# One expert's first matrix loaded by two transfers of 4 MB instead of four of 2 MB

## The reference

```python
u = hf[toks] @ w1[e] + b1[e]            # w1[e]: 1024 x 2048 f32, 8 MB
g_, lin = u[:, :D_FF], u[:, D_FF:]
y = ((lin + 1.0) * g_ * jax.nn.sigmoid(SWIGLU_ALPHA * g_)) @ w2[e] + b2[e]   # w2[e]: 1024 x 1024 f32, 4 MB
```

## Time and profile before

| | |
|---|---|
| median of 3 runs | 1930.34 us (1930.14 to 1932.53) |
| the profiled execution's own time | 1930.87 us |
| its span | 1929.1 us |
| mean granted TensorE clock | 0.992 of full |
| PE busy | 1802.8 us, 93% of the span |
| DVE, ACT, POOL busy | 510.2, 252.6, 111.0 us |
| products with `w1` (L1071) | 2112, which is 33 passes of 64 |
| experts (from the first product with `w1` to the last with `w2`) | 243.97 to 1183.09 us |

### The profile page before, as it was taken

One profiled execution on the slowest core, in us unless ns is written; L12 is line 12 of the kernel. 1 busy time (PEld: TensorE's weight loads), 2 busy tenths in 40 slices (PEclk: granted clock), 3 DMA queues, 4 the chain that ended last, 5 costly groups with the idle time before them and its releaser, 6 DMA issues.

```text
span 1929.1 us, 21701 instructions
## 1 busy us (share of the span) xinstructions
PE 1802.8 (93%) x8583; PEld 1033.3 (54%) x8584; DVE 510.2 (26%) x1032; ACT 252.6 (13%) x519; POOL 111.0 (6%) x148
## 2 busy tenths in 40 slices
PE   6997899999999899899898898989999999899998
PEld 3445733333333233233233234867888888788887
DVE  1237432323222222222132123133110005611000
ACT  1125300110001000000010012013110003211000
POOL 4003600000000000000000001000000000200000
PEclk9998999999999999999999999999999999999999
DMA  9683399979999999999999998430333433444430
GB/s 374 259 264 115 128 405 428 429 305 428 427 429 428 428 429 427 428 429 428 428 428 428 429 428 338 149 113 34 141 131 136 166 135 110 152 153 146 160 131 22
DMA packets 93090, 547.36 MB, mean 284 GB/s; under 512 B 5906, under 2 KB 9186, under 8 KB 65298
## 3 DMA queue, kind: packets, MB, share of 16 engines
q1 hardware_dynamic: 92850, 545.75, 70.2%
q10 hardware_dynamic: 192, 0.92, 0.2%
HBM read 545.60 MB, written 1.05 MB: 283 GB/s over the span
## 4 chain that ended last, share of the span: by engine, by line
PE 62%; DMA 31%; DVE 4%; SPq 1%; issue 1%; ACT 1%; POOL 1%; DVEq 0%; POOLq 0%; ACTq 0%
DMA ring<-in_exp_w 30%; PE ps L1131 20%; PE ps L1230 12%; PE ps L1071 12%; PE ps L753 4%; PE ps L1102 4%; PE ps L943 1%; PE ps L1025 1%; PE ps L1043 1%; PE ps L1265 1%; PE ps L1182 1%; DMA ring<-in_w_in 1%; PE ps L711 1%; DVE arena L2000 1%; SPq L475 0%
## 5 line engine op out<-in xcount | busy, mean ns | idle before, releaser
L1071 PE MATMUL ps<-ring,arena 128*64 128x512 f32 x2112 | 473.9, 595 | 56.5 <-DMA ring<-in_exp_w 56.4
L1131 PE MATMUL ps<-hn,ring 128*128 128x272 f32 (+1 forms) x1536 | 346.5, 388 | 0.0
L1071 PEld LDWEIGHTS ps<-ring,arena 128*64 128x64 f32 x2112 | 148.1, 137 | 362.6 <-issue 240.5
L1131 PEld LDWEIGHTS ps<-hn,ring 128*128 128x128 f32 x1536 | 291.8, 190 | 53.3
L1102 PE MATMUL ps<-arena 128*64 128x512 f32 x1056 | 233.9, 595 | 3.5
L1230 PE MATMUL ps<-arena,ring 128*128 128x272 f32 (+1 forms) x1024 | 228.5, 386 | 1.1 <-DVE arena L1950 1.1
L1230 PEld LDWEIGHTS ps<-arena,ring 128*128 128x128 f32 x1024 | 194.3, 190 | 35.0 <-DVE arena L1950 1.9
L1102 PEld LDWEIGHTS ps<-arena 128*64 128x64 f32 x1056 | 75.2, 137 | 140.9 <-issue 140.6
L1311 ACT ACTIVATE arena<-ps 128x512 f32<-128x512 f32 (+2 forms) x135 | 71.1, 535 | 402.9 <-PE ps L1102 212.2
L1851 DVE TENSOR_SCALAR arena<-ps 128x512 f32<-128x512 f32 x33 | 22.8, 691 | 364.9 <-PE ps L1071 364.9
L1763 DVE TENSOR_SCALAR arena<-arena,rstd 128x64 f32<-128x64 f32 x68 | 18.3, 311 | 304.2 <-PE ps L1071 303.5
(11 more groups left out here) (365 smaller groups left out, 1196.6 us busy)
## 6 DMA issues: line engine op xcount, KB each, us to landing
ring<-in_exp_w SPq DMA_DIRECT2D x128, 2048.0 KB, 24.8
arena<-in_exp_w SPq DMA_DIRECT2D x64, 2048.0 KB, 21.8
ring<-in_mlp_w_up SPq DMA_DIRECT2D x16, 2048.0 KB, 7.5
ring<-in_mlp_w_down SPq DMA_DIRECT2D x16, 2048.0 KB, 7.7
ring<-in_ada_w SPq DMA_DIRECT2D x12, 2048.0 KB, 12.6
ring<-in_sb_w_qkv SPq DMA_DIRECT2D x6, 2048.0 KB, 14.0
ring<-in_w_in SPq DMA_DIRECT2D x5, 2048.0 KB, 9.6
ring<-in_lru_w_in SPq DMA_DIRECT2D x4, 2048.0 KB, 7.9
```

The lines of the kernel that those rows point to most:

```text
L1071: last = mm(bank(2 + part)[64 * h:64 * h + 64, :], lhs, w[:, k % 2, at:at + 512], start=False, stop=(k == C - 1))
L1131: last = mm(bank((n0 + q) % 8)[:, lo:TT], w[:, k, P * q:P * q + P], act[:, k, lo:TT], start=(k == 0), stop=(k == C - 1))
```

## The change

The first matrix of an expert comes in two parts of 512 rows (4 MB). Partition p gets four neighbouring rows in one run of 32 KB, across two neighbouring slots of the ring. So that the two slots of a part stand side by side, the attention block's loads begin at slot 3 (`A_FIRST`), and the `w1` parts begin at slot 0. A part is issued when both quarters of it have been read, PE waits once for each part, and the gathered tokens are ordered in fours instead of twos. `w2` is as it was; its loads are now parts 2 and 3, and both wait for `wout_done` 8 in the case of expert 0, as before.

```diff
-PASS_LOADS = 6
+A_FIRST = 3
+PASS_LOADS = 4
...
-A_AT, A_AMOUNT = slot_amounts(A_LOADS, 0, [0] * RING)
-B_AT, _ = slot_amounts(B_LOADS, A_N, [n + 16 * EXPERTS for n in A_AMOUNT])
+A_AT, A_AMOUNT = slot_amounts(A_LOADS, A_FIRST, [0] * RING)
+assert (A_FIRST + A_N) % RING == 0
+B_AT, _ = slot_amounts(B_LOADS, 0, [n + 16 * EXPERTS * (r % 2 == 0) for r, n in enumerate(A_AMOUNT)])
...
-    return ("w1_parts", p * 4 + (part + 1)) if part < 4 else ("w2_parts", p * 2 + (part - 3))
+    return ("w1_parts", p * 4 + 2 * (part + 1)) if part < 2 else ("w2_parts", p * 2 + (part - 1))
...
-        if part < 4:
-            r = (A_N + part) % RING
-            src = a["exp_w1"][0, ds(expert, 1), 2 * P * part:2 * P * (part + 1), :]
-            sp.dma_start(m.ring[:, r, :], src.rearrange("e (p k) n -> p (e k n)", p=P)).then_inc(s.loaded[r], 16)
+        if part < 2:
+            src = a["exp_w1"][0, ds(expert, 1), 4 * P * part:4 * P * (part + 1), :]
+            dst = m.ring[:, 2 * part:2 * part + 2, :].rearrange("p r n -> p (r n)")
+            sp.dma_start(dst, src.rearrange("e (p k) n -> p (e k n)", p=P)).then_inc(s.loaded[2 * part], 16)
...
-        if part < 4:
-            wait_for(a_freed(A_N + part - RING))
-        elif part == 4:
+        if part < 2:
+            wait_for(a_freed(A_N + 2 * part - RING))
+            wait_for(a_freed(A_N + 2 * part + 1 - RING))
+        elif part == 2:
             sp.wait_ge(s["wout_done"], C)
...
-            r = (A_N + kk) % RING
-            pe.wait_ge(s.loaded[r], expert * 16 + (A_AMOUNT[r] + 16))
-            w = m.ring[:, r, :].rearrange("p (k n) -> p k n", n=2 * FF)
+            if kk % 2 == 0:
+                pe.wait_ge(s.loaded[kk], expert * 16 + (A_AMOUNT[kk] + 16))
+            w = m.ring[:, kk, :].rearrange("p (k n) -> p k n", n=2 * FF)
...
-            copy(h2.rearrange("p (a k d) -> p a d k", a=2, k=2),
-                 bank(4 + 2 * t + half).rearrange("p (a d k) -> p a d k", a=2, k=2), "h2_placed")
+            copy(h2.rearrange("p (k d) -> p d k", k=4),
+                 bank(4 + 2 * t + half).rearrange("p (d k) -> p d k", k=4), "h2_placed")
...
-    v.tensor_copy(m.sh_row.rearrange("p (a k d) -> p a d k", a=2, k=2),
-                  bank(3).rearrange("p (a d k) -> p a d k", a=2, k=2)).then_inc(s["sh_read"], 1)
+    v.tensor_copy(m.sh_row.rearrange("p (k d) -> p d k", k=4),
+                  bank(3).rearrange("p (d k) -> p d k", k=4)).then_inc(s["sh_read"], 1)
```

More of the change, by code:

```diff
@@ L478, in load_part @@
     def load_part(part, expert):
-        if part < 4:
-            r = (A_N + part) % RING
-            src = a["exp_w1"][0, ds(expert, 1), 2 * P * part:2 * P * (part + 1), :]
-            sp.dma_start(m.ring[:, r, :], src.rearrange("e (p k) n -> p (e k n)", p=P)).then_inc(s.loaded[r], 16)
-        else:
-            src = a["exp_w2"][0, ds(expert, 1), 512 * (part - 4):512 * (part - 3), :]
-            sp.dma_start(m.w2[:, part - 4, :],
-                         src.rearrange("e (p k) n -> p (e k n)", p=P)).then_inc(s.w2_loaded[part - 4], 16)
+        if part < 2:
+            src = a["exp_w1"][0, ds(expert, 1), 4 * P * part:4 * P * (part + 1), :]
+            dst = m.ring[:, 2 * part:2 * part + 2, :].rearrange("p r n -> p (r n)")
+            sp.dma_start(dst, src.rearrange("e (p k) n -> p (e k n)", p=P)).then_inc(s.loaded[2 * part], 16)
+        else:
+            src = a["exp_w2"][0, ds(expert, 1), 512 * (part - 2):512 * (part - 1), :]
+            sp.dma_start(m.w2[:, part - 2, :],
+                         src.rearrange("e (p k) n -> p (e k n)", p=P)).then_inc(s.w2_loaded[part - 2], 16)
     for part in range(PASS_LOADS):
-        if part < 4:
-            wait_for(a_freed(A_N + part - RING))
-        elif part == 4:
+        if part < 2:
+            wait_for(a_freed(A_N + 2 * part - RING))
+            wait_for(a_freed(A_N + 2 * part + 1 - RING))
+        elif part == 2:
             sp.wait_ge(s["wout_done"], C)
```

## The result

The changed kernel takes 1942.57 us (median of 7 runs, 1940.01 to 1949.04), the kernel before 1932.53 us (7 runs, 1930.14 to 1938.5). The ratio is 1.0055, with an interval of 1.0036 to 1.0074: slower by 10 us, where 10.6 were forecast. (The forecast counted from 1930.34 us, the median of three executions, and so gave 1940.9.)

The account below looks back on a forecast made before the run. The experts' stage was taken as bound by the DMA transfers, delays at restart and end counting one for one. 1.4 + 3.43 + 3.43 + 3.43 - 2.1 + 1.0 = +10.6 us gave 1940.9 us, range 1935 to 1944.5.

Parts of the forecast that it names:

- experts' start: First experts' loads: third quarter issued later with the fourth, delaying loads behind it to expert 1's end; +1.4 us.
- half behind expert 5's landing: First pass of expert 5: 32 products instead of 16 stand behind its last landing; +3.43 us.
- restart after the double pass: Expert 5's second pass: first ring place comes free after 32 products, not 16, so the load queue restarts later; +3.43 us.
- half behind the last landing: Experts' end: 7.08 us of products instead of 3.65 behind the last landing of `w1`; +3.43 us.
- speed of the stream: Expert loads: fewer packets at 4.3 ns each save 0.07 us an expert, over 31 first matrices; -2.1 us.
- longer last packet: Landings of experts 5 and 31: 16 KB more in the last packet costs 0.5 us each; +1.0 us.
- Rival 3: After expert 5: late restart hidden by PE's waitless stretch from 406 to 545; 1932.2 us; chance 0.04.
- a sign of being wrong: Forecast is wrong if restart doesn't move, queue runs dry in steady state, or cadence moves over 0.1 us.
- rival 2: Expert stream and kernel get faster; tie at 0.41 us saved a matrix, 1913.6 us at 450 GB/s; chance 0.05.
- rivals 1 and 4: Expert loads: 1, runs cut into 16 KB packets, 1942.0 us, chance 0.17; 4, longer runs stream worse, 1973, 0.04.
- one wait of about 2.9 us: PE's steady-state pass: one wait of about 2.9 us replaces two of 1.2; priced at nothing.

Follow-up runs that it names:

- half-only kernel: Kernel before with its 2 MB transfers, but first-matrix quarters waited for and given back in pairs; 1948.29 us, ratio 1.0078.
- the kernel with three products in the wait: Changed kernel plus three unused 128x256 products in every pass ahead of the wait for the second half; 1940.51 us, ratio 1.0040 against the kernel before.

## Why the prediction was right

The part of its mechanism that decides the sign held: one piece twice as large is paid for at three places. The sum held too, 10.6 us against 10.73, but so close a hit is luck. Inside the sum two errors each way cancel: one cost missed and one too small (4.2 us together), one gain too small and one cost that isn't there (4.0 together).

| term | forecast | measured | from |
|---|---|---|---|
| experts' start | +1.4 | +2.15 | expert 5's landing, halves with old transfers |
| half behind expert 5's landing | +3.43 | +3.43 | same, 7.09 against 3.65 |
| restart after the double pass | +3.43 | +3.43 | 422.16 - 393.77 - 8.78 = 19.61, before 410.45 - 390.62 - 3.65 = 16.18 |
| half behind the last landing | +3.43 | +3.43 | same as above; undone by quarters for expert 31 |
| speed of the stream | -2.1 | -5.1 | -4.16 from restart to last landing, -0.94 before |
| longer last packet | +1.0 | 0 | 12.1 us against 12.3 |
| clock behind a wait of 2.6 us | none | +3.4 | 8.78 us for 7.1, twice |

**The experts' start.** The forecast took the stream as unbroken at expert 1's first half, and it was: issued at 253.0 and landed 14.2 us later, 9.8 behind the load before it. Most of the 0.75 us that were missing lies ahead of that, at expert 0's second half of `w2`. It landed 11.5 us behind the experts' first product (235.0 + 22.4 = 257.4, against 245.91), where the forecast had 10.9 (254.9 against 243.97).

**The restart carries to the end.** Rival 3 (the late restart is hidden by PE's stretch without a wait) fell: the stream was unbroken from 422.16 to 1174.88, and the half-only kernel paid all of it.

**The queue stayed full in the steady state**, and the longest wait was 2.63 us where near 2.9 was said.

**The step that failed most is "the stream's speed".** The 4.3 ns a packet was drawn from the 408 GB/s of 2 KB runs and carried on to 32 KB; the cadence of 4 MB in one run and in two gives 9.0 ns. What a packet of 2 KB costs was no measure for halving the number of 16 KB ones. At 9.0 ns the 31 matrices give 31 x 0.144 = 4.5 us. Most of the rest of the 5.1 is the restart's load, which landed 12.1 us and not 12.6 after its issue. The forecast named a cadence moved by over 0.1 us as a sign of being wrong, and it moved by 0.14: by its own sign this term was wrong, though the total was not.

The forecast set the Trainium skill's figure ("DMA: Bandwidth & Descriptors", Bandwidth: some 10.5 ns a packet) against the rows and turned it down. The 9.0 ns measured lie nearer to that figure than to the 4.3 of the rows.

The saving stayed far below the 0.41 us a matrix that rival 2 needed for a tie; rivals 1 and 4 fell with the packet count and the 431 GB/s.

**The step that is missing is the clock.** The text says that one wait of about 2.9 us takes the place of two of 1.2 and prices it at nothing. In the steady state that is so (the cadence is 29.24 us with falls and 29.23 without). Behind the two landings that set the time, it added 1.67 us each. Whether it falls at just those two passes is a matter of the execution: in the profile of the half-only kernel it fell at neither, in that of 4 MB in two runs at the last alone, and with quarters for expert 31 not at expert 5. How much the falls add to the medians stays open, for there is one profile of each kernel.

**The longer last packet** rested on 0.2 us between two landings of different loads. The forecast had 12.6 to 13.1 us for the restart's load; it landed in 12.1 here and in 12.2, 12.2 and 12.5 in three profiles of the experiments with the same load, and in 12.3 with runs of 16 KB.

## What to carry to other kernels

Where a stream of transfers is the bound, look for the places at which it restarts and at which it ends: each piece's size is paid there once, in the time that the consumer needs for it, and no steady state shows it. Bigger pieces in the steady middle and small ones at start, refill and end take the gain without the price. And where two short waits of TensorE merge to one long one, look at what stands behind it, for a part of it may run at half the clock.

## What the runs showed of the hardware

- Runs of 32 KB per partition went as one packet each and streamed at 431 GB/s against 428 with runs of 16 KB; 4 MB transfers of 16 KB runs stayed at 428. The saving is 9.0 ns for each packet fewer on a DMA engine.
- TensorE's granted clock fell to its lower level behind 11 of 16 waits of 2.6 us and behind none of 11 waits of 1.07 to 1.84 us in the changed kernel; it did behind 10 and 11 of 16 (2.4 to 2.7 us) in the two other kernels with halves throughout, and behind 9 of 12 in the one with halves in the middle. After each fall the next wait was below 2 us. In the kernel with three products in the wait, all 20 were below 1.2 us and the clock stayed full.
